# mLSTM with two chunks of 512 queries joined by one state, and the divisions of a head behind all its units

## The reference

```
b = cumsum(log_f);  dmat[t, s] = b[t] - b[s] + log_i[s] for s <= t, else -inf
m[t] = max(max_s dmat[t, s], b[t] + m_carried)
s[t, s] = (q[t] . k[s]) * exp(dmat[t, s] - m[t])
h[t] = sum_s s[t, s] v[s] / max(|sum_s s[t, s]|, exp(-m[t]))
y = sigmoid(o) * h
```

## Time and profile before

| | us |
|---|---|
| median of 3 runs | 2993.38 |
| lowest, highest | 2993.10, 2995.12 |
| span of the profiled execution | 2994.8 |
| mLSTM block, first projection to the merge's first matmul (1805.1 to 2185.2) | 380.1 |
| one head, second and third | 95.0 |

### The profile page before, as it was taken

One profiled execution on the slowest core, in us unless ns is written; L12 is line 12 of the kernel. 1 busy time (PEld: TensorE's weight loads), 2 busy tenths in 40 slices (PEclk: granted clock), 3 DMA queues, 4 the chain that ended last, 5 costly groups with the idle time before them and its releaser, 6 DMA issues. The chain is left out here.

```text
span 2994.8 us, 37617 instructions
## 1 busy us (share of the span) xinstructions
PE 2862.1 (96%) x14023; PEld 2269.2 (76%) x14023; DVE 1866.5 (62%) x2932; ACT 1297.7 (43%) x2039; POOL 578.4 (19%) x377
## 2 busy tenths in 40 slices
PE   7999998999999999899999999999999998999999
PEld 4766675778887777577898888777878776888886
DVE  6455687778877478746555022644352337999997
ACT  4355634642223242434444211222221226899995
POOL 1000020000002455210000221221122111544443
PEclk9999999999999999999999999999999998999999
DMA  6000063664445756413012222100222225778774
GB/s 249 29 22 15 8 246 148 199 220 160 163 147 205 282 182 249 166 54 119 24 31 78 70 71 78 56 28 28 91 72 70 100 107 189 259 268 273 256 262 169
DMA packets 116407, 407.32 MB, mean 136 GB/s; under 512 B 23556, under 2 KB 29988, under 8 KB 104736
## 3 DMA queue, kind: packets, MB, share of 16 engines
q1 hardware_dynamic: 82104, 348.82, 32.3%
q10 hardware_dynamic: 16440, 39.98, 3.7%
q0 software_dynamic: 17712, 16.52, 2.5%
HBM read 402.05 MB, written 82.66 MB: 162 GB/s over the span
## 5 line engine op out<-in xcount | busy, mean ns | idle before, releaser
L646 PE MATMUL psum<-ff_g,ffo_w_split 128*128 128x512 f32 x1056 | 253.3, 400 | 17.6 <-POOL ffo_w_split L566 11.1
L566 POOL TENSOR_TENSOR ffo_w_split<-ffo_w_raw,ffo_w_split 128x352 fp32r<-128x352 f32 x120 | 135.7, 1162 | 610.2 <-ACT ffo_w_split L511 610.2
L646 PEld LDWEIGHTS psum<-ff_g,ffo_w_split 128*128 128x128 f32 x1056 | 201.1, 192 | 64.9 <-POOL ffo_w_split L566 14.8
L4122 DVE TENSOR_TENSOR ex_g_lo<-ex_g_raw,ex_g_hi 128x1024 fp32r<-128x1024 f32 x188 | 220.9, 1216 | 1.2 <-ACT ex_g_hi L4059 1.1
L1027 PE MATMUL psum<-fi_t_sum_hi,fi_w_sum 128*128 128x512 f32 x704 | 220.2, 389 | 0.0
L4059 ACT CAST ex_g_hi<-ex_g_raw 128x1024 fp32r<-128x1024 f32 x188 | 191.9, 1053 | 1.9 <-PE psum L4002 1.9
L1027 PEld LDWEIGHTS psum<-fi_t_sum_hi,fi_w_sum 128*128 128x128 f32 x704 | 132.1, 188 | 27.4
L4000 PE MATMUL psum<-ex_g_hi,ex_x_hi 128*128 128x512 f32 x376 | 151.0, 402 | 0.0
L4002 PE MATMUL psum<-ex_g_hi,ex_x_lo 128*128 128x512 f32 x376 | 147.1, 391 | 0.0
L4001 PE MATMUL psum<-ex_g_lo,ex_x_hi 128*128 128x512 f32 x376 | 147.1, 391 | 0.0
L1027 PE MATMUL psum<-fi_t_sum_lo,fi_w_sum 128*128 128x512 f32 x352 | 136.9, 389 | 0.0
(11 more groups left out here) (645 smaller groups left out, 7677.6 us busy)
## 6 DMA issues: line engine op xcount, KB each, us to landing
ex_g_raw<-in_w_experts_gu_dram SPq DMA_DIRECT2D x32, 2048.0 KB, 8.8
ex_d_raw<-in_w_experts_d_dram SPq DMA_DIRECT2D x32, 1024.0 KB, 9.0
fi_raw<-in_ffn_in_dram SPq DMA_DIRECT2D x22, 1024.0 KB, 5.4
ffo_w_raw<-in_ffn_out_dram SPq DMA_DIRECT2D x31, 704.0 KB, 6.7
wom_w<-in_mod_w_dram SPq DMA_DIRECT2D x8, 2048.0 KB, 8.3
fi_first_raw<-in_ffn_in_dram SPq DMA_DIRECT2D x22, 512.0 KB, 4.6
ff_g<-fi_g SPq DMA_DIRECT2D x43, 256.0 KB, 2.0
ml_raw<-in_w_ml_dram SPq DMA_DIRECT2D x16, 512.0 KB, 4.4
```

The lines of the kernel that those rows point to most:

```text
L566: last = nc.gpsimd.tensor_tensor(w_lo[:, v % 2, cols], w_raw[:, v % 2, cols], w_hi[:, v % 2, cols].bitcast(F32), ALU.subtract)
L646: mm = nc.tensor.matmul(chip.psum[:, 2 * u + h, :], w[:, v % 2, k * P:(k + 1) * P], (a[u] if isinstance(a, tuple) else a)[:, c * n_kc + k, ...
L4122: nc.vector.tensor_tensor(cols(g_lo, n), cols(raw.g_raw[i % 3], n), cols(g_hi, n).bitcast(F32), ALU.subtract).then_inc(q["g_lo_made"], 1)
```

## The change

Both halves become chunks of their own: 8 units, widths 512, 384, 256, 128 twice. The keys of the first chunk reach the second through one state of 128 x 258 (256 value features, two columns of ones for n). TensorE transposes k's four blocks (`turn_keys`) behind `token_major`, VectorE scales them by exp(g - M at the chunk's end) (`kw`), and TensorE sums them with v into a state (`sum_keys`, between the two gate tiles). In unit 4 two matmuls apply the state to the scaled queries `qs` (`earlier`), and the first add of that half becomes a scalar_tensor_tensor that takes in qs times the state's column of ones.

All ten division steps of a head with a successor stand behind its last unit, first those of half 0; in the last head the first three of half 0 stand behind units 4 to 6 and the rest in the merge's block, there between VectorE's subtraction of tiles 0 to 5 and of tiles 6 and 7. The halving goes: `GateRows` stores the floor row doubled and the sums are doubled in the two steps that read them. The gates are written into y's own tiles. TensorE's waits for y become waits for the quotients (`t_made`); score(0) waits for the first gate tile only. Weight roundings move to units 2, 4 and 6.

```diff
 class LateHalves(Halves):
+    READY = 6
...
     def on_act(self, act, second=None):
         for k in range(self.n_k):
             if k == self.between:
                 second()
+            if k == self.READY:
                 act.wait_ge(self.y_made, 4 * XH + 1)
...
+    def on_pe(self, pe, slot, k, part):
+        if (slot, k, part) == (self.slot, 0, 0):
+            pe.wait_ge(self.divided, 4 * XH + 1)
+        super().on_pe(pe, slot, k, part)
+
     def on_dve(self, dve):
-        for step in self.steps:
-            step(dve, XH - 1, 1)
-        super().on_dve(dve)
+        self.divide(dve, XH - 1, 0)
+        self.subtract(dve, range(0, self.READY))
+        for step, half in self.steps:
+            step(dve, XH - 1, half)
+        self.subtract(dve, range(self.READY, self.n_k))
...
             act.wait_ge(step, 14)
+            nc.scalar.activation(r[:, T, :], r[:, T, :], ACT.Identity, scale=2.0).then_inc(step, 1)
+            act.wait_ge(step, 15)
...
-    UNITS = [(c, j) for c in range(2) for j in range(4 * c + 4)]
+    UNITS = [(c, PER * c + i) for c in range(N_CH) for i in range(PER)]
...
-    steps = (floor_den, den, invert, divide, halve, write_y)
+    first_steps, last_steps = (floor_den, den, invert), (divide, write_y)
...
+            nc.gpsimd.memset(v[:, :, VW:SW], 1.0).then_inc(s_["later_made"], 1)
...
+                    if n == 6:
+                        act.wait_ge(s_["args_made"], h + 1)
+                        nc.scalar.activation(wk[:], args[:], ACT.Exp).then_inc(s_["wk_made"], 1)
...
+                for c in range(1, N_CH):
+                    nc.scalar.activation(qs[:, c - 1, :], m_row[:, c * CW:(c + 1) * CW], ACT.Exp, scale=-1.0,
+                                         bias=m_row[:, c * CW - 1:c * CW]).then_inc(s_["eq_made"], 1)
...
-                    if more and u in (4, 6):
-                        split_tile(h + 1, (4, 6).index(u))
-                    if more and u == 8:
+                    if more and u in (2, 4):
+                        split_tile(h + 1, (2, 4).index(u))
+                    if more and u == 6:
                         split_v(h + 1)
...
+                for b in range(KEYS):
+                    v_.tensor_scalar(kw[:, b, :], chip.psum[:, 6, b * P:(b + 1) * P], wk[:, b:b + 1], None, ALU.mult)\
+                        .then_inc(s_["kw_made"], 1)
+                dve.wait_ge(s_["eq_made"], STATES * h + STATES)
+                scaled = qs[:].rearrange("p c t -> p (c t)")
+                v_.scalar_tensor_tensor(scaled, qk[:, 0, CW:S], 0.25 * P ** -0.5, scaled, ALU.mult, ALU.mult).then_inc(s_["qs_made"], 1)
+                state(h, 0)
...
+                    elif u % PER == 0:
...
+                        nc.vector.scalar_tensor_tensor(wsum[:, half, cols], qs[:, c - 1, :], st[:, c - 1, VW:VW + 1], wt[:, u % 2, 0:w],
+                                                       ALU.mult, ALU.add).then_inc(s_["added"], 1)
...
-                    if 4 <= u < 4 + len(steps):
-                        steps[u - 4](dve, h, 0)
+                    if not more and HALF_UNITS <= u < HALF_UNITS + len(first_steps):
+                        first_steps[u - HALF_UNITS](dve, h, 0)
                 if more:
-                    for step in steps:
-                        step(dve, h, 1)
+                    for half in range(2):
+                        for step in first_steps + last_steps:
+                            step(dve, h, half)
...
                 project_tile(0)
-                pe.wait_ge(s_["y_made"], 4 * h + 1)
+                pe.wait_ge(s_["t_made"], 4 * h + 1)
                 project_tile(1)
                 pe.wait_ge(s_["v_lo_made"], h + 2)
+                pe.wait_ge(s_["t_made"], 4 * h + 3)
                 token_major(chip, pe, h_hi, h_lo, v_hi, v_lo, KD, VW,
...
+                turn_keys()
+                pe.wait_ge(s_["pre_made"], 2 * h + 1)
+                project_tile(2)
                 pe.wait_ge(s_["v_ready"], NB * h + NB)
-                pe.wait_ge(s_["gate_made"], 2 * h + 2)
+                pe.wait_ge(s_["later_made"], 2)
+                sum_keys(0)
+                pe.wait_ge(s_["pre_made"], 2 * h + 2)
+                project_tile(3)
+                pe.wait_ge(s_["gate_made"], 2 * h + 1)
                 for u in range(NU + 1):
                     if u < NU:
...
+                        score(u)
+                    if u == 1:
+                        pe.wait_ge(s_["gate_made"], 2 * h + 2)
                     if u >= 1:
                         x = u - 1
...
+                        if x % PER == 0 and x > 0:
+                            earlier(x // PER)
+                        apply(x)
```

```diff
+                def turn_keys():
+                    for b in range(KEYS):
+                        mm = nc.tensor.transpose(chip.psum[:, 6, b * P:(b + 1) * P], qk[:, 1, b * P:(b + 1) * P],
+                                                 chip.ident[:])
...
+                def sum_keys(c):
+                    pe.wait_ge(s_["kw_made"], KEYS * h + KEYS)
+                    for b in range(PER * c, PER * c + PER):
+                        mm = nc.tensor.matmul(chip.psum[:, STATE_BANK, 0:SW], kw[:, b, :], v[:, b, :],
+                                              start=(b == PER * c), stop=(b == PER * c + PER - 1))
...
+                def earlier(c):
...
+                    for i in range(XV):
+                        nc.tensor.matmul(sums_of(i, half)[:, cols], st[:, c - 1, i * P:(i + 1) * P], qs[:, c - 1, :],
+                                         start=True, stop=False)
```

More of the change, by code:

```diff
@@ L3133, in write_y, with sums_of @@
-    def write_y(dve, h, c):
-        dve.wait_ge(s_["t_made"], 6 * h + 3 * c + 3)
-        for i in range(XV):
-            nc.vector.scalar_tensor_tensor(tile_of(y, XV * h + i)[:, c * HALF:(c + 1) * HALF],
-                                           gate[:, i, c * HALF:(c + 1) * HALF], 1.0, t1[:, i, :],
-                                           ALU.add, ALU.mult).then_inc(s_["y_made"], 1)
-    steps = (floor_den, den, invert, divide, halve, write_y)
+    def sums_of(i, half):
+        return chip.psum[:, 2 + 3 * half + i, :]
@@ new lines, in in_half, with m_end, floor_den @@
+    def in_half(u):
+        return u // PER, slice(CW - width(u), CW)
+    def m_end(first, n):
+        return m_row[:].rearrange("p (c t) -> p c t", c=N_CH)[:, first:first + n, CW - 1:CW]
+    def floor_den(dve, h, half):
+        dve.wait_ge(s_["applied"], NU * h + HALF_UNITS * (half + 1))
+        dve.wait_ge(s_["totalled"], 2 * h + half + 1)
+        nc.vector.scalar_tensor_tensor(rc[:, 0, :], sums_of(XV, half), -2.0, e_row[:, half * HALF:(half + 1) * HALF],
+                                       ALU.mult, ALU.max).then_inc(s_["den_made"], 1)
@@ new lines, in den, with invert, divide @@
+    def den(dve, h, half):
+        dve.wait_ge(s_["den_made"], 4 * h + 2 * half + 1)
+        nc.vector.scalar_tensor_tensor(rc[:, 0, :], sums_of(XV, half), 2.0, rc[:, 0, :], ALU.mult, ALU.max).then_inc(s_["den_made"], 1)
+    def invert(dve, h, half):
+        dve.wait_ge(s_["den_made"], 4 * h + 2 * half + 2)
+        nc.vector.reciprocal(rc[:, 1, :], rc[:, 0, :]).then_inc(s_["rc_made"], 1)
+    def divide(dve, h, half):
+        dve.wait_ge(s_["rc_made"], 2 * h + half + 1)
+        for i in range(XV):
+            nc.vector.tensor_tensor(t1[:, i, :], sums_of(i, half), rc[:, 1, :], ALU.mult).then_inc(s_["t_made"], 1)
@@ new lines, in score @@
+                def score(u):
+                    c, j = UNITS[u]
+                    w = width(u)
+                    if u >= 2:
+                        pe.wait_ge(s_["weighted"], NU * h + u)
+                    nc.tensor.matmul(chip.psum[:, u % 2, 0:w], qk[:, 1, j * P:(j + 1) * P], qk[:, 0, j * P:j * P + w],
+                                     start=True, stop=True).then_inc(s_["scored"], 1)
+                def earlier(c):
+                    pe.wait_ge(s_["st_made"], STATES * h + c)
+                    pe.wait_ge(s_["qs_made"], h + 1)
+                    half, cols = in_half(PER * c)
+                    for i in range(XV):
+                        nc.tensor.matmul(sums_of(i, half)[:, cols], st[:, c - 1, i * P:(i + 1) * P], qs[:, c - 1, :],
+                                         start=True, stop=False)
@@ L3328, in _, with apply @@
+                def apply(u):
+                    c, j = UNITS[u]
+                    half, cols = in_half(u)
+                    pe.wait_ge(s_["weighted"], NU * h + u + 2)
+                    for i in range(XV):
+                        mm = nc.tensor.matmul(sums_of(i, half)[:, cols], v[:, j, i * P:(i + 1) * P], wt[:, u % 2, 0:width(u)],
+                                              start=(u == 0), stop=(u % PER == PER - 1))
+                    mm.then_inc(s_["applied"], 1)
                 pe.wait_ge(s_["weighted"], NU * h + 1)
@@ L3361, in _ @@
                                              start=True, stop=True).then_inc(s_["totalled"], 1)
-    return steps, s_["y_made"]
```

(6 more changed lines are left out.)

130 lines of the change are left out of this document (61 added, 69 removed).

## The result

| | before | changed |
|---|---|---|
| median, us | 2993.24 | 2972.16 |
| lowest, highest | 2992.45, 2995.12 | 2962.02, 2977.03 |

The ratio is 0.9924, 95% interval 0.9903 to 0.9945: 21.1 us less where 23.6 were forecast, 2972.16 where 2969.8 was. The profiled execution was the slowest of the four (2977.03, span 2975.3). So two things need an account: where 19.5 us of its span went, and why it lies 5 us above the median of the four.

A forecast was written before the change was run, and what follows sets the result against it. TensorE was taken to bound the mLSTM stage: 21.3 us from three heads plus 5.3 from the last, minus 3.0 in the merge, gives 23.6 off 2993.4, so 2969.8 us; range 2963 to 2983.

The forecast's parts named there:

- step 1: Old unit phase of a head with a successor: 27.8 us, of which matmuls 24.9 and waits 2.9, 1.2 the gate.
- step 2: New unit phase's matmuls: 16.3 us; twelve of 0.86 us go (10.3), two come (1.7).
- step 3: Unit phase waits: 1.2 us at first weighted tile, 0.6 at first total, 0.3 at unit 6; phase 18.4, 9.4 less.
- step 4: TensorE work added before the units: key sums 1.7 us, transposes 0.5, together 2.3 with issue.
- step 5: VectorE's and ScalarE's additions before the units cost nothing beside the projections; uncovered, about 3 us a head.
- The divisions behind the units: Divisions after the last unit: y_made 13.8 us into the next head instead of 9.0; cost nothing, 2 us of slack.
- The last head: Last head: reciprocal exposed, unit 7's tile 2.6 us late; phase 20.1 against 27.7, net gain 5.3 us.
- The merge: Merge after the last head: late y_made delays GpSimd's weight subtraction; loss 1.5 to 4 us, 3.0 taken, low end 0.5.
- Late loads: Rival: loads behind y_made land late, TensorE stands in token_major; 12 us over three heads, time 2982; 14%.
- the small units at the chain's pace: Rival: short units expose GpSimd's holds in full, up to 6.5 us more in three heads; 2980; 8%.
- The clock fell: Rival: unit waits drop the granted clock to 0.50, time 3035, 3%; one drop at the last head only, about 3 us.
- four signs of being wrong: Periods above 91 us, TensorE waiting on ml_v or ml_lo, granted clock under 1.00 in units, or no merge stall.

The follow-up runs named there:

- experiment 2: Changed kernel without the state (no transposes, scaled keys, key sum or state matmuls; later queries miss the first chunk's keys): 2959.13 us.
- experiment 4: Changed kernel with score(0) waiting for both gate tiles again: 2971.48 us.
- experiment 7: Changed kernel with ScalarE making the exponentials of units 0 and 1 ahead of the second gate tile: 2965.86 us.
- experiment 9: Changed kernel with early exponentials, last head's reciprocal behind unit 5, merge's divisions before its subtraction, and next value weights rounded behind unit 7: 2970.93 us.
- experiment 10: Changed kernel with the reciprocal of half 1 done twice in every head, more VectorE work ahead of y: 2974.93 us.
- experiment 3: Old kernel with both halves' divisions moved behind the last unit in the three heads with a successor: 2993.42 us.
- experiment 5: Changed kernel with floor, max and reciprocal of half 0 behind units 4 to 6 in every head: 2981.65 us.
- again: The changed kernel rerun without edit, five rounds, in a second batch: 2968.43 us, ratio 0.991.

## Why the prediction was right, step by step

*Matmuls (steps 1, 2).* Twelve go, two come: right. TensorE's busy 16.55 in the phase (16.3 counted). Counted as in the prediction, from the end of `project_tile(3)` (2053.76), the phase is 17.9 us against 18.4: 9.9 less than before, not 9.4. Period 87.3 against 87.8 (95.0 less 7.1 is 87.9).

*Waits (step 3).* Right in place: 1.33 in front of the first weighted tile (1.2), 0.23 at the first total (0.6), none at unit 6 (0.3). Three adds were held (0.81, 1.80 and 3.53 us), as counted; experiments 2, 4, 7 and 9 show how near unit 6 was. The gate's 0.5 was right at the front; that giving it up costs 1.1 (experiment 4) is unit 6 again.

*Added work (steps 4, 5).* 2.3 forecast; 1.9 from start to next start, 2.2 by what comes earlier without it (experiment 2). The transposes took 0.09 each, less than the router's row gave. VectorE's and ScalarE's additions cost nothing: no wait of TensorE names them.

*The divisions behind the units.* "Nothing" was right for the loads (y at 14.2, slack 2.0 us by experiment 10), but it left out a gain. I looked only for what the new place costs, not for what the old one did: 1.1 us a head in the old kernel (experiment 3), 3.3 or more in the new one (experiment 5). The matmul count already assumed that VectorE keeps up; the move is what made that so. Of the 2.9 us of waits in the old phase, step 1 named 1.2 and step 3 another 0.5; the rest, 1.2, is what experiment 3 gives back (1.1 to 1.4). The sum had it all the same, since the whole 27.8 us phase was taken as measured and no such stop was put into the new one; its cause was not named.

*The last head.* 5.3 forecast, 4.1 measured. Its stall was 2.0 and not 2.6, and a clock drop cost 1.2: from unit 7's values to the merge's first matmul 3.35 us, in experiment 7, with the same stall and no drop, 2.19. Without it the step gives 5.2, but its stall was 0.6 too large, so the agreement is partly luck.

*The merge.* 3.0 forecast, 3.2 measured, with GpSimd the releaser. The forecast's low end, 0.5 "if VectorE and GpSimd never collide", was wrong: here they did not (two subtractions of GpSimd took 4.79 us, 2.4 each), and the loss was 3.2. The length of the chain y, rounding, tanh, weights, subtraction sets it: 25.03 to 25.04 in the runs at full clock there (experiment 5) and at half clock (the changed kernel's), and experiment 10 moves it one for one.

*The rivals.* Late loads and the small units at the chain's pace did not happen (no wait on ml_lo or ml_v; 0.23 us). The clock fell at the last head, for 1.2 us of the 3 that I gave such a drop, and at the first head's start, for 1.6 (88.54 less 86.98). That is one of the four signs of being wrong, a granted clock under 1.00 in the units, in the last head's last unit alone; the other three did not show in the heads with a successor or in the merge (the last head's 91.4 us are over 91, of a forecast of 90.2). The Trainium skill's "TensorE: Matmul & The Clock Gate" (Part 1) has idleness drop the clock; the rows agree, but only for some stops: behind 2.01 us of standing the clock fell in three traces and stayed at 1.00 in four (experiments 2, 5, 7 and 10), and behind 2.74 us it fell twice out of three times (experiment 5).

*Sum.* 21.3 + 5.3 - 3.0 = 23.6 against 21.5 + 4.1 - 3.2 + 0.5 = 22.9 in the traces, less 3.4 before the stage. That 21.3 and 21.5 agree is luck: at full clock three heads give 3 x 7.67 = 23.0, so the forecast of 7.1 a head was 0.6 low, and the first head's half clock hid it. At full clock the traces' sum would be about 25.5; the two batches' medians gave 21.1 and 26.8.

## What to carry to other kernels

Where TensorE bounds a stage and a timeline shows its matmuls back to back, count matmuls at their pitch: the phase counted so was right to half a microsecond a head. Price a stop by the starts of the records around it, not by its idle time alone: 0.63 us of idle time were worth 1.2. When units get shorter, everything that the long ones covered must be found again: divisions between the units, a 3.4 us reciprocal among them, cost 1.1 us a head before and would cost 3.3 to 4.9 after. And a wait taken away at the front moves TensorE into the next engine's delay: read what is late next, as 1.0 us won there was worth 0.36 a head.

## What the runs showed of the hardware

**GpSimd's subtraction holds a VectorE add of two SBUF tiles until it ends**: POOL 2063.70 + 4.89 = 2068.59, the add ended at 2069.00 (3.53 instead of 0.56 us). The product that reads PSUM beside it (2064.88) took 0.56, as long as the one of unit 1, which had no GpSimd beside it (0.55). The Trainium skill, "SBUF — State Buffer", section "SBUF: two separate sides", has the two engines share a pair of ports by an exclusive lock for a whole instruction; the rows agree. Experiment 9 shows that moving the subtraction only chooses which add is held.

**The granted clock drops behind stops of TensorE, and not each time.** In the same code ahead of the stage 68 to 85 us ran at half clock, and the stage's start moved by 9 us. In the last head it dropped behind the 2.01 us wait in three traces (changed, again, experiment 4) and not in the four others with the same wait. Behind a stop of 1.88 us it dropped in one of three heads (experiment 9), behind 2.74 us in two of three (experiment 5). Two kernels that differ by 5 us need several executions, or the traces' periods, to be told apart. Whether the drop can be avoided without removing the stall was not tried.
